# Ten more pairs of column tiles by seven products, half-set sums spread over two blocks and stored from ScalarE's queue, in a gated four-branch layer (one core, Trainium2)

## The chip, the cores and the metric

The kernel runs on one core of one Trainium2 chip. The metric is the device time of one execution in microseconds (us); lower is better. The kernel before takes 2374.32 us, median of three runs (2374.21 to 2376.05).

## The reference, cut to what matters

```python
h = rmsnorm(x, g_pre[l])
proj = h @ w_in[l]                      # 1024 -> 12 parts of 512, and 4 x 1024 gate logits
(a_u, a_v, a_z, b_a, b_b, b_z, c_x, c_z, d_b, d_c, d_x, d_z, gate_logits) = jnp.split(proj, SPLITS, axis=-1)
v_n = layernorm(a_v, ...);  out_a = gmlp_spatial(a_u, v_n, w_s[l], b_s[l]) * silu(a_z)
out_b = silu(layernorm(causal_depthwise(b_a * sigmoid(b_b), conv_b_w[l]) + bias)) * silu(b_z)   # 31 taps
out_c = multiscale_pool(c_x) * silu(c_z)
out_d = d_b * causal_depthwise(d_c * d_x, conv_d_w[l]) * silu(d_z)                              # 3 taps
gates = sigmoid(gate_logits + b_gate[l])
merged = sum of gates[i] * (out_i @ w_branch[l, i]) over the four branches
y = merged @ w_out[l];  x = x + rmsnorm(y, g_post[l])
```

There is one layer, 2048 prompt tokens and 64 sample tokens, everything in float32. The tail of each state (conv, pool, short conv) and v_n of the sample are outputs too.

## The kernel before, in words

**Blocks and passes.** The 2048 tokens are worked in four blocks of 512; the last carries the 64 sample tokens as well, 576 columns. (The title of the change counts blocks from one: its blocks one and two are `j` = 0 and 1 here.) Every float32 operand is split into a high and a low part of type float32r, and each product takes three matmul passes: high by high, high by low, low by high.

**Units.** A block is 120 units in twelve sections (`SECTIONS`): B 8, V 4, C 8, M 8, G0 16, D 16, G1 16, G2 12, Z 4, G2b 4, G3 16, O 8. A full unit is one 128-column output tile of the input projection, 8 k tiles by 3 passes = 24 matmuls of 512 columns (48 of 288 in the last block). In a gated section (name with G) even units are gate logits, full; odd units are half units, 12 matmuls with a branch weight. `run_unit` (L1925) does a unit. Units alternate between the two PSUM halves `acc[:, 0]` and `acc[:, 1]`, and a unit waits until its half is emptied (`acc_free`): for gate units by ScalarE's sigmoid (L843), for half units by VectorE's merge (L1506).

**Weights.** In block 0 SyncE loads raw weights, ScalarE casts the high part (L776), GpSimd subtracts the low part (L643), and SyncE stores both in DRAM (`split_main`, `split_branch`). In later blocks SyncE loads the split weights into a ring of four (L502), each load issued when the unit four before it is done.

**Seven products.** In blocks 2 and 3 pairs of output tiles are worked as 2 by 2 block products in Strassen's manner (`seven_pairs`, `product`, L2146): 7 products of 12 matmuls with half the columns each, in place of two full units. `PAIRS` lists them: 25 per block, in G0 (the last three of four), D, G1, G2, Z, G3. The four partial sums of a pair are put together by VectorE (`pair_sums`, L1539 to L1554) in the tiles `zc`, beginning with a copy by ScalarE (`copy_p1`, L801). In D every odd pair stands in the `side` PSUM banks, the other pairs in `acc`. A product whose bank is used again waits for the sum that empties it: the sixth product of a pair waits for the first sum of the same pair.

They need sums on both sides. **Weight side, half sets:** each pair has two half sets, so 50. In block 1 SyncE loads a half set (L568), GpSimd makes four sums (L658 to L663; `s_half`), ScalarE casts the high part (`s_cast`, L787), GpSimd subtracts the low part (L666), and SyncE stores 1 MB in `s_parts` (L573). There are two output buffers, so the sums of a half set wait for the store of the one two before it, and three raw buffers. The tables `HALF_LOAD`, `HALF_CAST`, `HALF_STORE` and `HALF_POOL` say at which unit or pair of units each step stands in each engine's order. **Token side:** `t_sums` (L1406 to L1410) makes t1 to t4 from `h_hi` and `h_lo` by ten VectorE operations between the results of section M, ScalarE casts them (`t_cast`, L792), VectorE subtracts (`t_low`, L1418); the first pair waits for each.

**Order.** All orders are written out by hand. VectorE also works the 31 taps of the depthwise conv, one `conv_step` (L1197) of four operations (eight in the last block) at a time, put in wherever the code calls it. In block 0 SyncE, GpSimd and, in the gated sections, ScalarE run loops.

```python
HALF_LOAD = [h * 29 // 25 for h in range(NH)]
HALF_CAST = [max(0, 2 * s - 1) for s in HALF_LOAD]
HALF_STORE = [s + 2 for s in HALF_LOAD]
```

Of the kernel before, what the change touches and what calls it, by code (L numbers as in the profile page):

```python
# [19 lines left out]
P = 128  # L20
# [31 lines left out]
SEVEN = [("G0", 3), ("D", 8), ("G1", 4), ("G2", 4), ("Z", 2), ("G3", 4)]  # L52
PAIRS = [(n, q) for n, c in SEVEN for q in range(c)]
PAIR_TILE = [MAIN0["G2b"] if (n, q) == ("G2", 3) else MAIN0[n] + 2 * (q + (n == "G0")) for n, q in PAIRS]
# [5 lines left out]
SEVEN_AT = UNIT0["G0"] + 4  # L60
SEVEN_UNITS = UNIT0["O"] - SEVEN_AT
SEVEN_SIGS = 42
# [23 lines left out]


def half_unit(u):

    r = u % UPB  # L90
    return any(n[0] == "G" and UNIT0[n] <= r < UNIT0[n] + c and (r - UNIT0[n]) % 2 for n, c in SECTIONS)
# [40 lines left out]
def chunk_stream():  # L132
# [7 lines left out]
    for j in range(SEVEN0, NBLK):  # L140
        if j > SEVEN0:
            for name, count in SECTIONS:
                for r in range(4 if name == "G0" else count):
# [4 lines left out]
                if name == "G0":  # L148
                    break
        for p, (name, q) in enumerate(PAIRS):  # L150
# [4 lines left out]
            if name[0] == "G":  # L155
                srcs += [("branch", GATED[name][0] * KT + 2 * (q + (name == "G0")) + t, 0) for t in range(2)]
# [17 lines left out]
def build(nc, x_t, x_rows, w_main, w_half, w_branch, cols, rows, bs_rows, ws_t, mask_t, pool_w, ident_in,  # L174
# [82 lines left out]
    tmp = sb("tmp", [P, WMAX])  # L257
    diag_hi = sb("diag_hi", [P, BLK // P + 1, P], F32R)
# [5 lines left out]
    lnv_g_bc, lnv_b_bc = w_raw[0][:, 0:WB], w_raw[0][:, WB:2 * WB]  # L264
# [18 lines left out]
    for j in range(SEVEN0, NBLK):  # L283
        hw = (WMAX if j == NBLK - 1 else BLK) // 2
        part = CT * hw * 4
        if j == NBLK - 1:
            t_at = [raw_at, raw_at + part, xr_at, raw_at + 2 * part] + [xr_at + n * part for n in (1, 2, 3)] + [bs_at]
        else:
            t_at = [raw_at + n * part for n in range(4)] + [xr_at + n * part for n in (2, 3, 0, 1)]
# [197 lines left out]
    def _(sp):  # L487
        def raw_load(u, r, src, n):

            if not isinstance(u, int) or u >= RING:  # L490
                sp.wait_ge(w_lo_done, u - RING + 1)
            sp.dma_start(w_raw[r % RING][:, 0:n], src).then_inc(w_landed[r % RING], 16)

        def split_store(u, r, dst, n):

            sp.wait_ge(w_lo_done, u + 1)
            sp.dma_start(dst, f(w_pair[r % RING])[:, :, 0:n]).then_inc(split_stored[r % RING], 16)
# [18 lines left out]
        raw_load(0, 0, raw_rows(MAIN0["B"]), DM)  # L516
        load_x(sp, 0)

        for name, count in SECTIONS:
            u0 = UNIT0[name]  # L520
            prev = [n for n, _ in SECTIONS][max(0, [n for n, _ in SECTIONS].index(name) - 1)]

            def store_before(u, r, i):

                if i > 0 or not isinstance(i, int):
                    owner, m0 = name, i * 4 - 4
                elif name == "B":
# [24 lines left out]
            body(0)
            if name == "B":
# [1884 lines left out]
```

## Time and profile before

| what | value |
|---|---|
| median of the runs | 2374.32 us |
| the profiled execution: its own time | 2372.68 us |
| its span | 2370.9 us, 34948 instructions |
| PE (TensorE) busy | 2353.2 us, 99% |
| VectorE, GpSimd, ScalarE busy | 1563.9 (66%), 639.9 (27%), 442.7 us (19%) |
| PE in the chain that ended last | 92% |
| mean DRAM traffic | 290 GB/s |
| SyncE's DMA queue, ScalarE's DMA queue | 652.18 MB, 32.49 MB |

How to read it: PE is busy nearly all the time and its granted clock is full throughout, so the time is the sum of PE's instructions and of the few places where it stands still. Another engine matters only where it makes PE wait.

### The profile page before, as it was taken

Reading aid. Unit: us, or ns where it says so; the run is one execution under the profiler, and the core shown is the slowest. Engines: PE = TensorE matmul, PEld = TensorE weight load, DVE = VectorE, ACT = ScalarE, POOL = GpSimd, SP = SyncE. Lnnn points to the kernel's source line nnn. Section 1 sums busy time; section 2 is a strip of 40 time slices with the busy share of each in tenths; the row PEclk is TensorE's granted clock in tenths of the full one; section 3 lists DMA queues with packets and bytes.
Section 4 is the critical chain, followed back from the end, with each engine's and each line's share of the span. In section 5 each row is a group of like instructions: output and inputs, shape, how many; then the busy total and the mean of one; then the engine's idle time right before and its main releaser. Section 6 shows DMA issues by size and latency. Waiting matters only on the chain.

```text
span 2370.9 us, 34948 instructions
## 1 busy us (share of the span) xinstructions
PE 2353.2 (99%) x13240; PEld 2086.4 (88%) x13240; DVE 1563.9 (66%) x2349; ACT 442.7 (19%) x646; POOL 639.9 (27%) x423
## 2 busy tenths in 40 slices
PE   9999999999999999999999999999999999999998
PEld 7888888888888888788888899999899999999998
DVE  7886886854666578875276856776337786577643
ACT  5222222323112111121101100111110110010111
POOL 4534544455645646666200000000100000000000
PEclk9999999999999999999999999999999999999999
DMA  8877879788987988999764699999774458988884
GB/s 329 321 248 278 309 258 328 279 289 335 394 323 286 359 327 328 379 340 361 287 242 179 214 327 369 311 326 326 269 252 161 159 187 286 331 282 268 279 282 176
DMA packets 220673, 686.62 MB, mean 290 GB/s; under 512 B 18096, under 2 KB 19760, under 8 KB 186736
## 3 DMA queue, kind: packets, MB, share of 16 engines
q1 hardware_dynamic: 207920, 652.18, 76.9%
q10 hardware_dynamic: 12608, 32.49, 3.7%
q8 instruction: 93, 1.52, 0.2%
q14 instruction: 52, 0.43, 0.1%
HBM read 514.14 MB, written 170.46 MB: 289 GB/s over the span
## 4 chain that ended last, share of the span: by engine, by line
PE 92%; DVE 5%; DVEq 1%; DMA 1%; issue 1%; ACT 0%; POOL 0%; POOLq 0%; SPq 0%; ACTq 0%
PE acc L1925 50%; PE acc L2146 18%; PE side L2157 7%; PE side L2069 4%; PE side L2146 4%; PE acc L2306 3%; PE side L2306 3%; DMA w_pair<-split_main 1%; PE acc L2303 1%; PE side L2303 1%; PE side L2097 1%; PE side L2087 1%; DVE t_sum L1410 0%; PE acc L2336 0%; DVE cb L1197 0%
## 5 line engine op out<-in xcount | busy, mean ns | idle before, releaser
L1925 PE MATMUL acc<-h_hi,w_pair 128*128 128x512 f32 x2752 | 864.2, 390 | 3.5 <-DMA w_pair<-split_main 3.4
L1925 PEld LDWEIGHTS acc<-h_hi,w_pair 128*128 128x128 f32 x2752 | 516.7, 188 | 111.4 <-issue 3.8
L1925 PE MATMUL acc<-h_lo,w_pair 128*128 128x512 f32 x1376 | 535.3, 389 | 0.0
L1197 DVE SCALAR_TENSOR_TENSOR cb<-glu,col,cb 128x512 f32<-128x512 f32 x600 | 425.5, 775 | 18.5 <-issue 10.5
L643 POOL TENSOR_TENSOR w_pair<-w_raw,w_pair 128x1024 fp32r<-128x1024 f32 x118 | 268.4, 2286 | 272.6 <-ACT w_pair L776 257.5
L675 POOL TENSOR_TENSOR rstd<-msq,nhalf 128x5 f32<-128x5 f32 (+4 forms) x19 | 19.9, 1047 | 1125.5 <-DVE msq L1107 531.8
L1925 PEld LDWEIGHTS acc<-h_lo,w_pair 128*128 128x128 f32 x1376 | 258.4, 188 | 53.4
L2146 PE MATMUL acc<-t_hi,chunk 128*128 128x256 f32 (+1 forms) x1344 | 266.9, 287 | 1.3 <-DVE merged L1502 1.3
L2146 PEld LDWEIGHTS acc<-t_hi,chunk 128*128 128x128 f32 x1344 | 216.6, 189 | 1.9 <-DVE merged L1502 1.7
L2146 PE MATMUL acc<-h_hi,chunk 128*128 128x256 f32 (+1 forms) x1008 | 205.0, 289 | 2.4 <-issue 1.3
L2146 PE MATMUL acc<-t_lo,chunk 128*128 128x256 f32 (+1 forms) x672 | 193.1, 287 | 0.0
L1925 PE MATMUL acc<-out_hi,w_pair 128*128 128x512 f32 x528 | 173.6, 390 | 0.0
L2146 PEld LDWEIGHTS acc<-h_hi,chunk 128*128 128x128 f32 x1008 | 164.5, 190 | 4.0 <-DVE zc L1539 1.8
L666 POOL TENSOR_TENSOR s_out<-s_sum,s_out 128x1024 fp32r<-128x1024 f32 x50 | 122.5, 2449 | 150.9 <-ACT s_out L787 148.8
L2157 PE MATMUL side<-out_hi,chunk 128*128 128x288 f32 (+1 forms) x720 | 162.0, 327 | 0.0
L1925 PE MATMUL acc<-h_hi,chunk 128*128 128x288 f32 x832 | 146.9, 297 | 0.0
L2146 PE MATMUL acc<-h_lo,chunk 128*128 128x256 f32 (+1 forms) x504 | 145.3, 288 | 0.0
L776 ACT ACTIVATE w_pair<-w_raw 128x512 fp32r<-128x512 f32 (+1 forms) x117 | 109.8, 940 | 94.6 <-PE acc L1925 65.2
L2146 PEld LDWEIGHTS acc<-t_lo,chunk 128*128 128x128 f32 x672 | 126.9, 189 | 0.2
L2157 PEld LDWEIGHTS side<-out_hi,chunk 128*128 128x128 f32 x720 | 116.3, 188 | 8.9
L1925 PEld LDWEIGHTS acc<-h_hi,chunk 128*128 128x128 f32 x832 | 123.0, 189 | 0.5
L1925 PEld LDWEIGHTS acc<-out_hi,w_pair 128*128 128x128 f32 x528 | 99.1, 188 | 21.0 <-DVE tmp L1506 0.3
(327 smaller groups left out, 3409.2 us busy)
## 6 DMA issues: line engine op xcount, KB each, us to landing
w_pair<-split_main SPq DMA_DIRECT2D x118, 1024.0 KB, 6.3
chunk<-split_main SPq DMA_DIRECT2D x226, 512.0 KB, 5.6
chunk<-s_parts SPq DMA_DIRECT2D x200, 512.0 KB, 6.0
split_main<-w_pair SPq DMA_DIRECT2D x88, 1024.0 KB, 6.4
s_parts<-s_out SPq DMA_DIRECT2D x50, 1024.0 KB, 5.8
w_raw<-in_w_main SPq DMA_DIRECT2D x88, 512.0 KB, 4.6
chunk<-split_branch SPq DMA_DIRECT2D x62, 512.0 KB, 4.4
s_raw<-in_w_half SPq DMA_DIRECT2D x50, 512.0 KB, 6.6
```

What stands on the lines that cost most here:

```text
L643: pool.tensor_tensor(w_lo[s][:, 0:n], w_raw[s][:, 0:n], f(w_hi[s])[:, 0:n], ALU.subtract).then_inc(w_lo_done, 1)
L666: pool.tensor_tensor(s_out[h % 2][:, :, 1, :], s_sum[h % 2][:, :, 1, :], f(s_out[h % 2])[:, :, 0, :], ALU.subtract).then_inc(s_lo_done, 1)
L776: act.activation(w_hi[s][:, 0:n], w_raw[s][:, 0:n], ACT.Copy).then_inc(w_hi_done, 1)
L1197: dve.scalar_tensor_tensor(dst, src, c1("conv_w", c * CK + t), dst, ALU.mult, ALU.add)
L1925: ins = pe.matmul(acc[:, s, b, 0:m], w_k[:, wt, wk], mv_[:, k, t0:t0 + m], start=(k == 0 and n == 0), stop=(k == nk - 1 and n == 2))
L2069: ins = pe.matmul(v_tile(t), ht[:, k, t * P:(t + 1) * P], w_k[:, wt, :], start=(r == 0 and n == 0), stop=(r == 3 and n == 5))
L2087: ins = pe.matmul(side[:, k % 2, t0:t0 + m], wt[:, c, :], part[:, c, t0:t0 + m], start=(n == 0), stop=(n == 2))
L2097: ins = pe.matmul(side[:, k % 2, t * P:t * P + n], v_n[0:n, t, c * P:(c + 1) * P], ws[0:n, c, 0:n], start=True, stop=True)
L2146: ins = pe.matmul(bank, w_k, rhs[r_part][:, k, :], start=(k == 0 and c == 0), stop=(k == CT - 1 and c == 2))
L2157: ins = pe.matmul(side[:, m % 2, t * 512:t * 512 + m_], wt[:, w_part, k * P:(k + 1) * P], rhs[:, k, t0:t0 + m_], start=(k == 0 and c == 0) ...
L2303: ins = pe.matmul(bank[:, 0:N1], wt[:, part, n * P:(n + 1) * P], act_part[:, TOK * P:WMAX], start=(k == 0 and c == 0), stop=(k == KT - 1 a ...
L2306: ins = pe.matmul(bank, act_part[:, n // 2 * P:(n // 2 + 1) * P], wt[n % 2][:, part, :], start=(k == 0 and c == 0), stop=(k == KT - 1 and ...
```

## The change

1. `SEVEN` gains section M (4 pairs) and the first pair of G0: 30 pairs per block, ten more over blocks 2 and 3. The eight units of M and the first four of G0 are no longer run there. `seven_m` works M's results; the gMLP side products (`m_job`) move between the third and fourth product of M's pairs; the pool side products (`p_job`) move ahead, after units 2, 3, 6 and 7 of C.
2. There are 60 half sets. Sixteen (`HALF0`) are made in block 0, one buffer set, every 10.5 half units; the other 44 in block 1, on 50 of 54 slots of two units, with four slots from `X_ROWS_AT` (units 78 to 85, in G2) left free.
3. Their stores are issued by ScalarE: in `s_cast`, at the unit after the slot, behind the cast that stands at the same unit.
4. `t_sums` now makes t1 to t4 from `h_x` at the end of the block before, four operations, ahead of the casts, the low parts and GpSimd's `h_lo`, which overwrites `h_x` and so waits for them. The low parts follow before the statistics of `y_nat`.
5. Conv steps of blocks 2 and 3: 8 in B, 3 in C, 8 in G0, one in each of the first three D results (19 to 21), then as before. Block 0's loops on SyncE, GpSimd and ScalarE are written out. t4's high part lives in another place in the last block, with one copy of it by ScalarE.

```diff
-SEVEN = [("G0", 3), ("D", 8), ("G1", 4), ("G2", 4), ("Z", 2), ("G3", 4)]
+SEVEN = [("M", 4), ("G0", 4), ("D", 8), ("G1", 4), ("G2", 4), ("Z", 2), ("G3", 4)]
...
-HALF_LOAD = [h * 29 // 25 for h in range(NH)]
-HALF_CAST = [max(0, 2 * s - 1) for s in HALF_LOAD]
-HALF_STORE = [s + 2 for s in HALF_LOAD]
-HALF_POOL = [2 * s for s in HALF_LOAD]
+HALF0 = 16
+X_ROWS_AT = UNIT0["G2"] // 2 + 1
+SLOTS = [s for s in range(54) if not X_ROWS_AT <= s < X_ROWS_AT + 4]
+HALF_SLOT = [SLOTS[h * len(SLOTS) // (NH - HALF0)] for h in range(NH - HALF0)]
+SUM0 = [unit_at(26 + h * 21 // 2) for h in range(HALF0)]
+CAST0 = [unit_at(START[u] + 2) for u in SUM0]
+LOW0 = [u + 1 for u in CAST0]
+LOAD0 = [unit_at(START[u] - 8) + 7 for u in SUM0]
+HALF_LOAD = LOAD0 + [UPB + 2 * s for s in HALF_SLOT]
+HALF_STORE = [u + 1 for u in LOW0] + [UPB + 2 * s + 1 for s in HALF_SLOT]
+HALF_CAST = CAST0 + [UPB + max(0, 2 * s - 1) for s in HALF_SLOT]
+RAW_OF = [0 if h < HALF0 else (h - HALF0) % 3 for h in range(NH)]
+SUM_OF = [0 if h < HALF0 else (h - HALF0) % 2 for h in range(NH)]
...
+        def s_store(h):
+            act.wait_ge(s_lo_done, h + 1)
+            act.dma_start(s_parts[h // 2, h % 2, :, :, :, :], f(s_out[SUM_OF[h]])).then_inc(s_stored[SUM_OF[h]], 16)
         def s_cast(j, u):
+            for h in range(NH):
+                if HALF_CAST[h] == u:
+                    out, b = s_out[SUM_OF[h]], SUM_OF[h]
+                    act.wait_ge(s_summed, h + 1)
+                    act.activation(out[:, :, 0, :], s_sum[b][:, :, 1, :], ACT.Copy).then_inc(s_hi_done, 1)
+            for h in range(NH):
+                if HALF_STORE[h] == u:
+                    s_store(h)
...
+        def t_sums(j):
+            if j == SEVEN0:
+                for b in range(2):
+                    dve.wait_ge(s_stored[b], 16 * SUM_OF.count(b))
+            dve.drain()
+            dve.tensor_tensor(t1, b12, b11, ALU.subtract).then_inc(t_summed, 1)
+            dve.tensor_tensor(t3, b12, b22, ALU.subtract).then_inc(t_summed, 1)
+            dve.drain()
+            dve.tensor_tensor(t2, b22, t1, ALU.subtract).then_inc(t_summed, 1)
+            dve.drain()
+            dve.tensor_tensor(t4, b21, t2, ALU.subtract).then_inc(t_summed, 1)
...
+            def seven_m(c):
+                p = PAIRS.index(("M", c))
+                pair_sums(p, lambda: m_side(c))
+                dve.tensor_tensor(tmp[:, 0:w], tmp[:, 0:w], zc[0][:, 0:w], ALU.mult)
+                dve.wait_ge(pair_sig, sigs_before(j, p) + 1)
+                dve.tensor_tensor(tmp[:, 0:w], tmp[:, 0:w], sig[0][:, 0:w], ALU.mult)
+                dve.tensor_tensor(tmp[:, 0:w], tmp[:, 0:w], zc[1][:, 0:w], ALU.mult)
+                dve.drain().then_inc(pair_used, 2)
+                result(j, 1, c)
...
+                if i < 3:
+                    conv_step(j, 19 + i)
                 pair_sums(p + 1)
```

**ScalarE, section G3 of block 1, before.** Each sigmoid empties a gate unit; between them stands the cast of a half set.

```order
L843 ACTIVATE sig_104<-acc,col 128x512 [waits sig_used,acc_done]
L787 ACTIVATE s_out_100<-s_sum_102 128x4x256 [waits s_summed]
L843 ACTIVATE sig_105<-acc,col 128x512 [waits sig_used,acc_done]
L787 ACTIVATE s_out_101<-s_sum_103 128x4x256 [waits s_summed]
L843 ACTIVATE sig_104<-acc,col 128x512 [waits sig_used,acc_done]
```

The same place in the changed kernel:

```order
L849 ACTIVATE sig_104<-acc,col 128x512 [waits sig_used,acc_done]
L786 ACTIVATE s_out_100<-s_sum_102 128x4x256 [waits s_summed]
L778 DMA s_parts<-s_out_101 128x2048 [waits s_lo_done]
L849 ACTIVATE sig_105<-acc,col 128x512 [waits sig_used,acc_done]
L786 ACTIVATE s_out_101<-s_sum_103 128x4x256 [waits s_summed]
L778 DMA s_parts<-s_out_100 128x2048 [waits s_lo_done]
```

The store of one half set now stands behind the cast of the next one.

**VectorE, last block, section D, between an even pair and the odd pair after it, in the changed kernel** (`ext`, `tmp`: the three taps; `cb`: the conv; `zc_110<-side,zc_111`: first sum of the odd pair). Before, the four `cb` rows shown (eight in all) were not there, and the first sum followed the copies.

```order
L1775 COPY halo_d<-ext_112 128x2
L1777 COPY smp_d<-ext_112 128x2
L1218 SCALAR_TENSOR_TENSOR cb<-glu,col,cb 128x512
L1218 SCALAR_TENSOR_TENSOR cb<-glu,col,cb 128x64
L1218 SCALAR_TENSOR_TENSOR cb<-glu,col,cb 128x512
L1218 SCALAR_TENSOR_TENSOR cb<-glu,col,cb 128x64
...
L1551 TENSOR_TENSOR zc_110<-side,zc_111 128x288 [waits chunk_done,p1_copied]
```

A conv step of eight operations has moved ahead of the odd pair's first sum.

**VectorE, end of block 1, in the changed kernel** (`h_x`: the scaled input of block 2; `y_nat`: this block's output, whose statistics came right after `h_x` before).

```order
L1142 SCALAR_TENSOR_TENSOR h_x<-h_x,col,h_row 128x512
L1176 TENSOR_TENSOR t_sum_1_148<-h_x 128x1024 [waits s_stored1,s_stored0]
L1177 TENSOR_TENSOR t_sum_3_154<-h_x 128x1024
L1179 TENSOR_TENSOR t_sum_2_151<-h_x,t_sum_1_148 128x1024
L1181 TENSOR_TENSOR t_sum_4_157<-h_x,t_sum_2_151 128x1024
L1164 TENSOR_TENSOR t_lo_3_153<-t_sum_3_154,t_hi_3_152 128x1024 [waits t_hi_done]
L1164 TENSOR_TENSOR t_lo_1_147<-t_sum_1_148,t_hi_1_146 128x1024 [waits t_hi_done]
```

The token sums have moved from section M of the block to the end of the block before it.

## Rows read from the trace of the kernel before

**Rows 1.** The page: each engine's busy time; engines of the chain.

```profile
PE 2353.2 (99%) x13240; PEld 2086.4 (88%) x13240; DVE 1563.9 (66%) x2349; ACT 442.7 (19%) x646; POOL 639.9 (27%) x423
...
PE 92%; DVE 5%; DVEq 1%; DMA 1%; issue 1%; ACT 0%; POOL 0%; POOLq 0%; SPq 0%; ACTq 0%
```

**Rows 2.** Stretches of time: A:B, us; busy of five engines; clock, DMA share, GB/s.

```profile
57.00:545.00 488.00, 487.62 (x2169) 403.89 (x2169) 358.55 (x399) 140.07 (x185) 237.31 (x109) 1.00 0.81 289
590.00:1125.00 535.00, 531.49 (x2362) 439.93 (x2361) 361.81 (x422) 102.89 (x135) 312.33 (x250) 1.00 0.91 344
1402.00:1481.00 79.00, 78.79 (x667) 78.58 (x666) 49.45 (x103) 5.62 (x12) 0.00 (x0) 1.00 1.02 368
```

**Rows 3.** The chain that ended last: start us, us, what.

```profile
1290.95 5.44 PE acc L1925 x24
...
1392.13 9.93 PE acc L2146 x84
...
1803.18 31.98 PE acc L1925 x240
...
1970.42 11.10 PE acc L2146 x84
```

**Rows 4.** Timeline of PE where it enters the pairs, blocks 2 and 3.

```profile
1344.90 0.35 PE L2146 MATMUL acc<-h_hi,chunk 128*128 128x256 f32 x1 [1.28 <-issue]
...
1348.58 0.38 PE L2146 MATMUL acc<-t_hi,chunk 128*128 128x256 f32 x1 [0.58 <-DVE merged L1502]
...
1938.35 0.40 PE L2146 MATMUL acc<-t_hi,chunk 128*128 128x288 f32 x1 [0.67 <-DVE merged L1502]
```

**Rows 5.** PE's timeline in block 1, where a split weight comes late.

```profile
985.58 0.47 PE L1925 MATMUL acc<-h_hi,w_pair 128*128 128x512 f32 x1 [3.37 <-DMA w_pair<-split_main]
```

**Rows 6.** Section D, timeline: PE enters an odd pair; VectorE at its first sum.

```profile
1421.74 0.28 PE L2146 MATMUL side<-h_hi,chunk 128*128 128x256 f32 x1
...
2021.09 0.29 PE L2146 MATMUL side<-h_hi,chunk 128*128 128x288 f32 x1
```

```profile
1425.59 0.42 DVE L1539 TENSOR_TENSOR zc<-side,zc 128x256 f32<-128x256 f32 x1
...
2025.70 0.45 DVE L1539 TENSOR_TENSOR zc<-side,zc 128x288 f32<-128x288 f32 x1
```

**Rows 7.** VectorE's timeline: a conv step in block 2 and in the last.

```profile
1304.43 2.74 DVE L1197 SCALAR_TENSOR_TENSOR cb<-glu,col,cb 128x512 f32<-128x512 f32 x4
...
1887.46 3.53 DVE L1197 SCALAR_TENSOR_TENSOR cb<-glu,col,cb 128x512 f32<-128x512 f32 x8
```

**Rows 8.** Timelines of GpSimd and ScalarE in G3 of block 1.

```profile
1099.31 2.39 POOL L666 TENSOR_TENSOR s_out<-s_sum,s_out 128x1024 fp32r<-128x1024 f32 x1 [2.19 <-DMA s_parts<-s_out]
1101.66 1.19 POOL L658 TENSOR_TENSOR s_sum<-s_raw 128x256 f32<-128x256 f32 x1
...
1105.02 0.74 POOL L663 TENSOR_TENSOR s_sum<-s_raw,s_sum 128x256 f32<-128x256 f32 x1
```

```profile
1105.76 0.69 ACT L843 ACTIVATE sig<-acc,col 128x512 f32<-128x512 f32 x1 [6.52 <-PE acc L1925]
1106.34 1.05 ACT L787 ACTIVATE s_out<-s_sum 128x1024 fp32r<-128x1024 f32 x1
```

**Rows 9.** Issue to landing: tile `s_out` from 1060 to 1125 us; DMAs issued 1196:1198.

```profile
DMA to landing us min/median/max: 5.0/6.2/8.7
```

```profile
w_pair<-split_main SPq DMA_DIRECT2D x1, 1024.0 KB, 6.0
out_y_rows<-x_half ACTq DMA_DIRECT2D x1, 1024.0 KB, 7.0
```

**Rows 10.** Start of block 2: the chain, and VectorE's timeline.

```profile
1168.53 43.54 PE acc L1925 x192
```

```profile
1146.99 2.45 DVE L1145 SCALAR_TENSOR_TENSOR h_x<-h_x,col,h_row 128x512 f32<-128x512 f32 x2 [1.39 <-DMA h_x<-in_x_t]
...
1307.25 1.23 DVE L1408 TENSOR_TENSOR t_sum<-h_hi 128x1024 f32<-128x1024 f32 x1
```

More of the change, by code:

```diff
@@ L142, in chunk_stream @@
             for name, count in SECTIONS:
-                for r in range(4 if name == "G0" else count):
+                if name == "M":
+                    break
+                for r in range(count):
                     u = j * UPB + UNIT0[name] + r
@@ L155, in chunk_stream @@
             if name[0] == "G":
-                srcs += [("branch", GATED[name][0] * KT + 2 * (q + (name == "G0")) + t, 0) for t in range(2)]
+                srcs += [("branch", GATED[name][0] * KT + 2 * q + t, 0) for t in range(2)]
             for src in srcs:
@@ L263, in build @@
     mean_wb = sb("mean_wb", [P, 2])
-    lnv_g_bc, lnv_b_bc = w_raw[0][:, 0:WB], w_raw[0][:, WB:2 * WB]
+    lnv_b_bc, lnv_g_bc = [zc[b][:, 0:WB] for b in range(2)]
     bs_at = at[0]
@@ new lines, in _ @@
+        units = [(name, r) for name, count in SECTIONS for r in range(count)]
+        for u, (name, r) in enumerate(units):
+            m = unit_pieces(name, r)[0][1]
+            if half_unit(u):
+                raw_load(u, raw_branch_rows(m), WB)
+            else:
+                raw_load(u, raw_rows(m), DM)
+            if u == 0:
+                load_x(sp, 0)
+            if u >= RING:
+                m = unit_pieces(*units[u - RING])[0][1]
+                if half_unit(u - RING):
+                    split_store(u - RING, split_branch_rows(m), WB)
+                else:
+                    split_store(u - RING, split_rows(m), DM)
+            sum_moves(u)
+            if u == RING - 1:
@@ L664, in s_half, with s_low, sum_steps @@
             pool.drain().then_inc(s_summed, 1)
+        def s_low(h):
+            out = s_out[SUM_OF[h]]
             pool.wait_ge(s_hi_done, h + 1)
-            pool.tensor_tensor(s_out[h % 2][:, :, 1, :], s_sum[h % 2][:, :, 1, :], f(s_out[h % 2])[:, :, 0, :],
+            pool.tensor_tensor(out[:, :, 1, :], s_sum[SUM_OF[h]][:, :, 1, :], f(out)[:, :, 0, :],
                                ALU.subtract).then_inc(s_lo_done, 1)
+        def sum_steps(step):
+            for h in range(NH):
+                if HALF_LOW[h] == step and h < HALF0:
+                    s_low(h)
+            for h in range(NH):
+                if HALF_SUM[h] == step:
+                    s_sums(h)
+                    if h >= HALF0:
+                        s_low(h)
         powers = [0]
@@ L734, in _ @@
             else:
-                for u in range(UNIT0["O"]):
+                for u in range(UPB):
                     if u == UNIT0["B"] + 1:
@@ L942, in _ @@
                 c = r // 4 * 2 + r % 2
+                if last and r == 2:
+                    act.wait_ge(vn_ready, j + 1)
+                    act.dma_start(v_s, lnv_g_bc[0:DEC, :]).then_inc(v_stored, 16)
+                if last and r == 3:
+                    act.wait_ge(v_stored, 16)
                 if r % 4 < 2:
@@ L955, in _ @@
             u0 = ub + UNIT0["M"]
-            for r in range(8):
+            for r in range(0 if is_seven(j) else 8):
                 u = u0 + r
@@ L1432, in _ @@
                 dve.drain().then_inc(side_free, 1)
+            for c in range(0 if is_seven(j) else CT):
+                u = ub + UNIT0["M"] + 2 * c
+                m_side(c)
                 ready_at(0, u // 2)
@@ L1442, in _ @@
                 result(j, 1, c)
[L1443 to L1449 removed]
+                if c % 2:
                     conv_step(j, 4 + c // 2)
@@ L1529, in merge @@
                 else:
-                    unrolled(dve, int(is_seven(j)), start, end, body)
+                    unrolled(dve, 0, start, end, body)
             def pair_sums(p, between=None):
```

389 lines of the change are left out of this document (162 added, 227 removed).

## The prediction

> **What bounds the kernel now.** I read the page first: PE is busy for 99% of the span and holds 92% of the chain; VectorE (66%), GpSimd (27%) and ScalarE (19%) are far from full [rows 1]. The granted clock is 1.00 in each stretch read [rows 2], so no change of clock enters the sum. Then the stretches of time: block 0's main part has 0.4 us without PE, block 1's has 3.5 us (535.00 less 531.49), section D of block 2 has 0.2 us [rows 2]. Then the chain, for what a unit and a pair cost PE: a full unit takes 5.44 us in block 2 and 31.98/5 = 6.40 us in the last block; a pair takes 9.93 and 11.10 us [rows 3]. The timelines give the stalls: 1.28 and 0.58 us where block 2 enters its first pair, 0.67 us in the last block [rows 4], and 3.37 us in block 1 where a split weight lands late [rows 5]. So the time is PE's instruction stream plus some 6 us of stalls. The change shortens the stream in blocks 2 and 3 and pays for it in block 1, in the chain that makes half sets.
>
> All sums start from the profiled execution's own time, 2372.68 us. The median of the runs is 1.64 us above it, and I add that at the end. 0.2% is 4.7 us, about what a measurement of this kernel can tell from no change.
>
> **Matmuls.** Four pairs of M and one of G0 replace ten full main tiles per block; branch matmuls (half as two products of the same columns) stay as they were. Block 2: 2 x 5.44 - 9.93 = 0.95 us a pair, five pairs, -4.8. Last block: 12.80 - 11.10 = 1.70, five pairs, -8.5 [rows 3]. Together **-13.2**.
>
> **Entry into the pairs.** Before, the first pair had to wait for token sums made in M and in the pair's own time: 1.28 + 0.58 us in block 2, 0.67 us in the last [rows 4], and small ones beside them of some 0.5 us in all (an estimate). Now the sums are made a block earlier. **-3.0**, at worst -1.0 if VectorE is what is late next.
>
> **Late weight in block 1.** Rows of x come in then beside half-set loads and stores, and PE stands 3.37 us [rows 5]. The four free slots take 6 MB out of just that stretch. **-3.5**, at worst 0.
>
> **Conv steps in D.** A step now stands ahead of an odd pair's first sum, and PE's sixth product waits for that sum. Last block: PE enters at 2021.09, so the sixth starts 5 x 11.10/7 = 7.93 us later, at 2029.0; the sum started at 2025.70 and takes 0.45 [rows 6]; behind a step of 3.53 us [rows 7] and some 0.15 us of gaps it ends at 2029.8. That is 0.8 us late, three times: 2.4. Block 2: needed at 1421.74 + 7.09 = 1428.8, done at 1425.59 + 2.74 + 0.42 + 0.15 = 1428.9 [rows 6, 7]: 0.1 x 3. **+2.7**; bounds 0 (VectorE reaches D earlier now that merges lie better) and 5.
>
> **Sixteen half sets in block 0.** Each is 4.10 us of sums (1101.66 to 1105.76) and 2.39 of low part on GpSimd and 1.05 on ScalarE [rows 8]. GpSimd: 237 + 16 x 6.5 = 341 of 488 us busy. DMA: 16 x 1.5 MB more, 289 + 52 = 341 GB/s, which is what block 1 carries now (344) with one stall [rows 2]. They have a single buffer and some 28 us each, so the store's time is hidden. What could show is a weight's low part waiting behind a sum: **+0.5**, bounds 0 and 5 (the bound by the 3.4 us stall of [rows 5]).
>
> **At no cost, and under what cover.** M's pairs take 9.93 us plus 0.89 of the side product; they read 7 x 0.5 MB in 10.8 us, 339 GB/s, under the 368 that D takes without stall [rows 2]; if that cover fails, 0.5 us a pair. VectorE drops ten sums per block (1.23 us and more each [rows 10]) for four, and loses conv steps in M to B and G0, where the gate units leave it room. At the block's end the sums follow the scaled input, which ends at 1149.4; four times 1.23 puts them at 1154.4, and GpSimd's low parts have until 1168.5, when PE begins the next block [rows 10]; if that is short, up to 5 us a block. Pool side products in C are ahead by one or two units, which their operands have as slack; 0 to 1 us.
>
> **The stores on ScalarE: the deciding term.** Follow one half set in block 1. ScalarE issues the store of half set h behind the cast of h+1. The sums of h+2 wait until that store has landed (two buffers), and the cast of h+2 waits for the sums. So one turn is cast, issue, landing L, 4.10 of sums, about 0.2 of signals: L + 4.3 us. Before, SyncE issued the store without waiting for any later cast, so this ring didn't exist; even so GpSimd once waited 2.19 us for a landing [rows 8]. Behind the cast on ScalarE stands the sigmoid that empties PE's half of PSUM. In gated sections a slot is 5.44 + 2.72 = 8.16 us of PE time [rows 3], so each slot puts the cast back by L + 4.3 - 8.16 = L - 3.86 us. In D and where full units stand a slot is 10.88 us and gives back 6.58 - L. A cast can be late by some 8.5 us before PE waits: it is due a slot ahead, 10.9 less the cast, the sigmoid and signals [rows 8]. In G3 seven slots stand on end; I take it 3.5 us late on entry and count five steps: 3.5 + 5(L - 3.86) - 8.5. In G1 and in G0 four steps: 4(L - 3.86) - 8.5 each.
>
> For L there are two rows near: the stores of this very stretch, issued by SyncE, took 5.0/6.2/8.7 us (least, median, most), and a 1 MB store on ScalarE's queue took 7.0 beside a 1 MB load of 6.0 [rows 9]. I take 6.3, nearest the median of the same stores. Then G3 gives 3.5 + 12.2 - 8.5 = 7.2, G1 1.3, and G0 about nothing, since a free slot lies nearer to it: **+8.5**. Bounds: L = 5.0 gives 1 (G3 alone, 0.7), L = 7.0 gives 22 (next part).
>
> A rule weighed against this: by the rows, SyncE's stores stand in the same queue as weight loads, and here the store may either pass them or share with them; 6.0 beside 7.0 is one case of sharing [rows 9]. The Trainium skill, page "DMA: Bandwidth & Descriptors", section "Issuing engines are not separate DMA queues", says that DMAs of any issuing engine run on the same 16 DMA engines and interleave, and that issuing from another one saves only issue time. By that rule the store gains nothing, and this case's pair of 6.0 and 7.0 us agrees.
>
> **Sum.** -13.2 - 3.0 - 3.5 + 2.7 + 0.5 + 8.5 = -8.0: 2364.7 on the profiled execution's base, **2366.3** on the median's.
>
> **Rivals.**
> - *A, short ring.* L is 5.4 or less since the store no longer stands behind queued weight loads. For: the least was 5.0 [rows 9]. Against: 344 to 368 GB/s of other traffic. Ring cost about 2: -14.5, **2360**. Chance 0.22.
> - *B, the forecast*, 2362 to 2370: 0.40.
> - *C, long ring, slower.* The store shares with a load in flight: 1 MB more at 344 GB/s is 3.0 us on top of 5.0, L up to 8.0. At L = 7.0 G3 gives 10.7, G1 and G0 4.1 each, and since 11.3 is above 10.88 the eight slots of D give nothing back and cost 0.4 each: 22, so **2380**. From L = 7.0 on it decides for slower than before by 0.2%. At L = 7.7 the same count gives 14.2 + 6.9 + 6.9 and 1.1 for each of eleven full slots: 40, **2398**. For: the 7.0 on that queue, the most of 8.7. Against: the median of 6.2. Chance 0.20. The rule of the page named above, read so that each store is slowed by the loads it now runs beside, is this case.
> - *D, traffic.* Ring short, but block 0 at 341 GB/s and M's pairs make PE wait for weights, 1 to 5 us more than I count, or the late weight of block 1 stays (+3.5) because the x rows alone cause it: **2370 to 2373**. Against: block 1 carried as much with one stall. Chance 0.13.
> - *E, matmul gain only.* Nothing waits anywhere: -19 and below, **2355**. Chance 0.05.
>
> **How the numbers follow.** The forecast is the likeliest case, B's middle. Faster by over 0.2% is below 2369.6: A, E, most of B: 0.60. Within: the top of B, D, the start of C: 0.18. Slower, over 2379.1: C from L = 7.0 on, and mishaps of VectorE at the new places: 0.22. The range goes from just under A's 2360 (2357) to C's beginning at L = 7.1 (2384), leaving out E and long rings, some 0.2.
>
> **What would show it.** Right: ScalarE waits for the sums (`s_sum`) in G0, G1 and G3 of block 1, GpSimd waits for `s_parts` before its sums, and PE waits for `sig` in G3 in steps of about 2.5 us; landing of `s_parts` near 6.3; pairs at 9.93 and 11.10 in M; stalls of 0.8 us before the sixth product of three odd pairs in the last block; no stall at 985 us and none at the first pair. Wrong: PE full in block 1's G3 (A or E), waits for `w_pair` or `chunk` (D), new idle time of PE in block 0 or at a block's start, none of which the sum has at more than 0.5 us.

## The result and the profile after

The changed kernel takes **2412.0 us** (median of four runs, 2409.4 to 2416.6) against 2374.3: the ratio is 1.0159, with an interval of 1.0146 to 1.0172. That is slower by 38 us where 8 us less was forecast, and outside the range (2357 to 2384). The profiled execution took 2416.6 us, its span is 2414.8.

The page of the kernel after, engines and chain, to be read beside [rows 1]:

```profile
PE 2362.4 (98%) x13360; PEld 2095.9 (87%) x13360; DVE 1602.1 (66%) x2407; ACT 447.1 (19%) x651; POOL 697.3 (29%) x473
...
PE 72%; DVE 9%; DMA 8%; POOLq 3%; issue 2%; POOL 2%; DVEq 2%; ACT 1%; ACTq 0%; SPq 0%
```

PE's busy time rose by 9.2 us where the shorter stream should have lowered it by 13.2. Its idle time rose from 17.7 (span less busy) to 52.4 us. DMA went from 1% to 8% of the chain, nearly all of it `s_parts<-s_out`, the landing of the half-set stores.

Where the time went, by the end of each block's output projection in PE's timeline (L2306 before, L2333 after):

| block | before, us | after, us | difference | predicted |
|---|---|---|---|---|
| 0 | 589.1 | 607.4 | +18.3 | +0.5 |
| 1 | 579.1 | 618.6 | +39.5 | +5.0 |
| 2 | 556.2 | 548.5 | -7.7 | -6.8 |
| last | 640.0 | 633.8 | -6.2 | -6.8 |

(Predicted: the terms put in their blocks. Block 1: -3.5 + 8.5. Block 2: -4.8, its entry -2.3, conv steps +0.3. Last block: -8.5, entry -0.7, conv steps +2.4.) Blocks 2 and 3 came as forecast. All of the error is in blocks 0 and 1, where the half sets are made.

What PE waited for in block 0 (first fence) and in block 1 (second): engine, line, releaser, us in total, times, longest.

```profile
PE acc L1949 <- DVE tmp L1518: 5.5, 2, 3.1
PE side L2111 <- DVE out_lo L1386: 3.9, 1, 3.9
```

```profile
PE acc L1949 <- ACT sig L849: 22.3, 7, 8.9
PE acc L1949 <- ACTq L942: 7.7, 2, 6.2
```

In block 1 PE stood 30.0 us, always for ScalarE; in block 0 it waited for VectorE. Counted back from the block's end by the time of a unit, the 30.0 us lie in five places: 7.7 at the results of V (L942), 5.0 in G0, 1.5 in G1, 8.9 in G2 and 6.9 in G3. Stretches of time (columns as in [rows 2]); the last two are the 14 us around and behind the end of the pause of 6.23 us in block 1:

```profile
57.00:545.00 488.00, 477.14 (x2087) 392.48 (x2088) 400.06 (x391) 147.81 (x192) 329.33 (x182) 0.99 0.87 325
...
590.00:1125.00 535.00, 511.15 (x2232) 420.47 (x2231) 316.61 (x403) 95.61 (x129) 256.79 (x215) 0.97 0.84 312
...
686.00:693.00 7.00, 6.04 (x14) 4.84 (x15) 2.67 (x4) 1.47 (x2) 5.77 (x6) 0.50 0.36 150
...
693.00:700.00 7.00, 7.00 (x32) 5.74 (x32) 6.30 (x10) 1.55 (x2) 3.09 (x2) 1.00 0.45 156
```

```profile
686.96 0.80 PE L1949 MATMUL acc<-h_hi,w_pair 128*128 128x512 f32 x1 [6.23 <-ACTq L942]
...
692.67 0.56 PE L1949 MATMUL acc<-h_lo,w_pair 128*128 128x512 f32 x1
...
693.52 0.40 PE L1949 MATMUL acc<-h_lo,w_pair 128*128 128x512 f32 x1
```

After the pause the granted clock is 0.50, the 1.2 GHz level, up to about 692.7 us, and back at 1.00, 2.4 GHz, behind it. A run of three 512-column matmuls takes 1.28 us at the low level (687.98 to 689.26) and 0.68 at the high one, so 5.7 us at the low level cost 2.7 us. The low stretches behind the eight pauses of 2.0 us or more last 3.3 to 5.9 us and so cost 1.6 to 2.8 us each, some 17 in all (an estimate from their lengths and the two rates). The mean clock is 0.97 over block 1 and 0.99 over block 0. Taken over the whole run PE's busy time is 2362.4 where 2353.2 - 13.2 = 2340.0 was due. Of these 22.4 us two or three are not the clock's: the same stream at full clock (the runs with ten and nine half sets in block 0 below) is busy for 2342.3 to 2343.5. **So 17 to 20 us went to the low clock behind the pauses**, beside 34.7 us of more idle time. That cost was in no term of the prediction.

Block 1's ring, in the timelines of GpSimd and ScalarE (ACTq is ScalarE's issuing) before the longest pause:

```profile
998.51 0.92 POOL L658 TENSOR_TENSOR s_sum<-s_raw 128x256 f32<-128x256 f32 x1 [4.58 <-DMA s_parts<-s_out]
...
1004.08 2.40 POOL L670 TENSOR_TENSOR s_out<-s_sum,s_out 128x1024 fp32r<-128x1024 f32 x1 [1.22 <-ACT s_out L786]
1012.00 0.75 POOL L658 TENSOR_TENSOR s_sum<-s_raw 128x256 f32<-128x256 f32 x1 [5.52 <-DMA s_parts<-s_out]
```

```profile
1002.94 1.06 ACT L786 ACTIVATE s_out<-s_sum 128x1024 fp32r<-128x1024 f32 x1 [7.77 <-POOLq L664]
1002.95 0.33 ACTq L778 DMA_DIRECT2D s_parts<-s_out  x1
...
1015.25 1.06 ACT L786 ACTIVATE s_out<-s_sum 128x1024 fp32r<-128x1024 f32 x1 [10.67 <-POOLq L664]
1015.26 0.33 ACTq L778 DMA_DIRECT2D s_parts<-s_out  x1
1015.63 1.46 ACTq L859 DMA_DIRECT2D x_half<-in_x_rows  x2
1017.12 4.39 ACTq L862 DMA_DIRECT2D x_dec<-in_x_rows  x4
1021.61 0.69 ACT L849 ACTIVATE sig<-acc,col 128x512 f32<-128x512 f32 x1 [5.30 <-issue]
```

```profile
1002.95 8.92 DMA s_parts<-s_out
```

```profile
1022.35 0.80 PE L1949 MATMUL acc<-h_hi,w_pair 128*128 128x512 f32 x1 [8.87 <-ACT sig L849]
```

The store is issued at 1002.95, behind the cast at 1002.94, and lands 8.92 us later; GpSimd waits 5.52 us for it, makes its sums, and only then the next cast can run at 1015.25. One turn is 12.31 us, the landing + 3.4, where PE's work for a slot is 8.16 (10.88 where full units stand, so even there nothing is given back). Behind that late cast ScalarE still has six issues of x rows (5.9 us), then the sigmoid at 1021.61 that lets PE go on. The rows of x that the free slots were to protect thus add to the lateness on ScalarE, where the prediction had looked at SyncE alone.

Landing of the stores, 610 to 1200 us:

```profile
DMA to landing us min/median/max: 3.9/8.3/11.5
```

Block 0, VectorE (first fence) and GpSimd beside it in the 10 us that end in PE's pause of 3.12 us:

```profile
339.83 8.07 DVE L1218 SCALAR_TENSOR_TENSOR cb<-glu,col,cb 128x512 f32<-128x512 f32 x4
348.25 0.69 DVE L1518 TENSOR_TENSOR tmp<-acc,sig 128x512 f32<-128x512 f32 x1 [0.34 <-issue]
```

```profile
340.49 2.39 POOL L643 TENSOR_TENSOR w_pair<-w_raw,w_pair 128x1024 fp32r<-128x1024 f32 x1 [3.50 <-ACT w_pair L770]
342.84 2.84 POOL L670 TENSOR_TENSOR s_out<-s_sum,s_out 128x1024 fp32r<-128x1024 f32 x1
345.64 1.71 POOL L643 TENSOR_TENSOR w_pair<-w_raw,w_pair 128x512 fp32r<-128x512 f32 x1
```

Four conv operations that take 2.74 us where GpSimd rests [rows 7] took 8.07 here: GpSimd's `s_out` operation of the half set stands between two of its own for the weights. The four took 0.75, 2.93, 2.88 and 1.75 us, and each of the last three ended 0.55 us behind the end of a GpSimd operation. In the same section of the kernel before such a step took 3.4:

```profile
336.51 3.42 DVE L1197 SCALAR_TENSOR_TENSOR cb<-glu,col,cb 128x512 f32<-128x512 f32 x4 [0.26 <-issue]
```

In section D of the last block, PE at the sixth product of odd pairs:

```profile
2048.72 0.40 PE L2174 MATMUL side<-h_hi,chunk 128*128 128x288 f32 x1 [0.63 <-DVE zc L1551]
...
2072.23 0.41 PE L2174 MATMUL side<-h_hi,chunk 128*128 128x288 f32 x1 [0.97 <-DVE zc L1551]
...
2095.40 0.40 PE L2174 MATMUL side<-h_hi,chunk 128*128 128x288 f32 x1 [0.62 <-DVE zc L1551]
```

The pauses at the entry of the pairs [rows 4] and the late weight [rows 5] are gone.

### The profile page after: what moved, and what is told of

It is laid out like the page before. It is cut to its first block, busy times and chain, and to the rows that moved or that the text cites. A ratio compares the mean times of both kernels' runs of the same rounds, so it can differ in the third digit from the quotient of the medians.

```text
span 2414.8 us, 34960 instructions
## 1 busy us (share of the span) xinstructions
PE 2362.4 (98%) x13360; PEld 2095.9 (87%) x13360; DVE 1602.1 (66%) x2407; ACT 447.1 (19%) x651; POOL 697.3 (29%) x473
## 4 chain that ended last, share of the span: by engine, by line
PE 72%; DVE 9%; DMA 8%; POOLq 3%; issue 2%; POOL 2%; DVEq 2%; ACT 1%; ACTq 0%; SPq 0%
PE acc L1949 28%; PE acc L2174 22%; PE side L2185 8%; DMA s_parts<-s_out 8%; PE side L2174 3%; PE side L2093 3%; PE acc L2333 2%; PE side L2333 2%; DVE cb L1218 2%; POOLq L659 1%; POOLq L664 1%; POOLq L662 1%; POOL s_sum L660 1%; PE side L2121 1%; PE acc L2330 1%
## 5 line engine op out<-in xcount | busy, mean ns | idle before, releaser
L1949 PE MATMUL acc<-h_hi,w_pair 128*128 128x512 f32 x2592 | 824.6, 394 | 30.9 <-ACT sig L849 22.5
L2174 PE MATMUL acc<-t_hi,chunk 128*128 128x256 f32 (+1 forms) x1520 | 300.6, 287 | 0.0
L2174 PE MATMUL acc<-h_hi,chunk 128*128 128x256 f32 (+1 forms) x1248 | 253.1, 289 | 0.4 <-DVE zc L1551 0.4
L2174 PE MATMUL acc<-t_lo,chunk 128*128 128x256 f32 (+1 forms) x832 | 239.3, 288 | 0.0
L2174 PEld LDWEIGHTS acc<-h_hi,chunk 128*128 128x128 f32 x1248 | 203.5, 190 | 1.2 <-DVE zc L1551 0.6
L670 POOL TENSOR_TENSOR s_out<-s_sum,s_out 128x1024 fp32r<-128x1024 f32 x60 | 152.7, 2545 | 94.7 <-ACT s_out L786 94.7
L2174 PE MATMUL acc<-h_lo,chunk 128*128 128x256 f32 (+1 forms) x624 | 179.9, 288 | 0.0
L2174 PEld LDWEIGHTS acc<-t_lo,chunk 128*128 128x128 f32 x832 | 157.1, 189 | 0.2
L2174 PEld LDWEIGHTS acc<-h_lo,chunk 128*128 128x128 f32 x624 | 118.2, 189 | 0.6
L1518 DVE TENSOR_TENSOR tmp<-acc,sig 128x512 f32<-128x512 f32 x48 | 33.2, 691 | 127.2 <-PE acc L1949 81.8
```

Of the source, the lines that this page charges most:

```text
L670: pool.tensor_tensor(out[:, :, 1, :], s_sum[SUM_OF[h]][:, :, 1, :], f(out)[:, :, 0, :], ALU.subtract).then_inc(s_lo_done, 1)
L1518: dve.tensor_tensor(tv(tmp, j), accv(1, j), tv(sig[r], j), ALU.mult).then_inc(acc_free[1], 1)
L1949: ins = pe.matmul(acc[:, s, b, 0:m], w_k[:, wt, wk], mv_[:, k, t0:t0 + m], start=(k == 0 and n == 0), stop=(k == nk - 1 and n == 2))
L2174: ins = pe.matmul(bank, w_k, rhs[r_part][:, k, :], start=(k == 0 and c == 0), stop=(k == CT - 1 and c == 2))
```

## The experiments

Each was timed in three rounds or more beside the kernel before (2374.3 to 2375.4 us). Block times come from PE's timeline as above.

### The store ahead of the next cast

```diff
-HALF_STORE = [u + 1 for u in LOW0] + [UPB + 2 * s + 1 for s in HALF_SLOT]
+HALF_STORE = [u + 1 for u in LOW0] + [UPB + 2 * s for s in HALF_SLOT]
```

> The changed kernel took 18.3 us more than before in block 0 (607.4 against 589.1), 39.5 more in block 1 (618.6 against 579.0), 7.7 less in block 2 and 6.2 less in block 3. Here the stores of block 1 stay on ScalarE's queue, but stand one unit earlier: at the unit of the slot itself, ahead of the next half set's cast instead of behind it. Block 0 is untouched. Ring theory (the store behind the next cast makes one half set wait for the landing of the last): the ring is cut, so PE's waits for sig (22.5 us) and the clock falls behind them go, block 1 takes 579 to 584 us, the kernel 2374 to 2380. Queue theory (the stores take 8.1 us on ScalarE's queue and the sums wait for the landing in any case): landing stays 8 us and block 1 stays over 605 us, the kernel over 2398.

Measured: 2372.95 us, ratio 0.9992 (0.9982 to 1.0001). Block 1 takes 577.1 us, block 0 still 607.6. Its store landing, 600 to 1200 us, and its stretch of block 1:

```profile
DMA to landing us min/median/max: 5.1/8.0/17.8
```

```profile
625.00:1170.00 545.00, 543.59 (x2414) 449.61 (x2414) 363.05 (x429) 98.26 (x132) 271.06 (x221) 1.00 0.87 327
```

One unit's shift of one instruction gives back 39 us. The landing is about as long as in the changed kernel (8.0 against 8.3 us at the median), and GpSimd still waits for it 19 times, but PE loses 1.4 us in the whole stretch. Queue theory falls: the length of the landing does nothing unless the ring makes it count.

### The stores back on SyncE

```diff
+            for h in range(HALF0, NH):
+                if HALF_STORE[h] == step:
+                    sp.wait_ge(s_lo_done, h + 1)
+                    sp.dma_start(s_parts[h // 2, h % 2, :, :, :, :], f(s_out[SUM_OF[h]])).then_inc(s_stored[SUM_OF[h]], 16)
```

(with `HALF_STORE` at 2 * (s + 2), in `sum_moves` of SyncE, and without them in `s_cast`)

> The changed kernel, but block 1's stores are issued by SyncE again, two slots behind as in the kernel before; block 0's stay on ScalarE. Ring theory: block 1 takes 579 to 584 us, as in the run with the store ahead of the cast, kernel 2374 to 2380, whatever the landing time is. Queue theory: landing falls from 8.1 to about 6 us here and here alone, and only this run loses the 39 us, the other keeps them. If both theories are wrong and 44 half sets beside other traffic are the cause, block 1 stays over 605 us in both.

Measured: 2373.87 us, ratio 0.9995 (0.9986 to 1.0005); block 1 takes 577.2 us. Landing:

```profile
DMA to landing us min/median/max: 4.1/5.6/12.7
```

Both halves of the theory hold, each by itself: the queue sets the landing (5.6 against 8.0 us), the order sets whether it costs. A pause of 1.16 us for a weight stands at 1002.6 us, with the four slots free.

### The ring, but on SyncE's queue

```diff
+                    if h + 1 < NH and HALF_CAST[h + 1] == HALF_CAST[h] + 2:
+                        sp.wait_ge(s_hi_done, h + 2)
```

(ahead of the wait for `s_lo_done` of the last experiment, `HALF_STORE` at 2 * s + 5)

> The changed kernel, with block 1's stores issued by SyncE but still held back until the next half set's cast is done (where the next slot follows at once): the ring of the change, on the other queue. Measured so far: landing in block 1 is 8.0 us on ScalarE's queue and 5.6 on SyncE's; cutting the ring takes 39 us out of block 1 on either queue. Ring with its length (one turn is landing + 4.3 us against 8.16 of PE's time a slot): at L = 5.6 three stretches are late by 4 or 5 slots of 1.7, at most 8.7 of the 8.5 that are free plus 3.5 in G3, so block 1 takes 579 to 588 us, kernel 2374 to 2384. Order-alone theory (a store behind the next cast costs what it cost, on whatever queue): block 1 stays over 605, kernel over 2398. SyncE held at the wait can also delay weights, which would show as PE waiting for w_pair.

Measured: 2383.14 us, ratio 1.0038 (1.0025 to 1.0050). Block 1 takes 585.7 us, 8.6 more than with the ring cut. Landing and PE's pauses in block 1:

```profile
DMA to landing us min/median/max: 4.7/4.9/15.4
```

```profile
951.86 0.50 PE L1955 MATMUL acc<-h_hi,w_pair 128*128 128x512 f32 x1 [1.34 <-DMA w_pair<-split_main]
...
996.26 0.50 PE L1955 MATMUL acc<-h_hi,w_pair 128*128 128x512 f32 x1 [3.27 <-ACT sig L855]
...
1005.15 0.47 PE L1955 MATMUL acc<-out_hi,w_pair 128*128 128x512 f32 x1 [1.55 <-DMA w_pair<-split_branch]
```

Against the block with the ring cut (577.1) the ring costs 9 us at a landing of 4.9 and 41 at 8.3 (618.6), and part of the 9 is SyncE, held at the new wait, bringing weights late (1.34 and 1.55 us). The turn behind the longest pause, from cast to cast on ScalarE:

```profile
981.32 1.06 ACT L792 ACTIVATE s_out<-s_sum 128x1024 fp32r<-128x1024 f32 x1 [6.62 <-POOLq L670]
...
991.67 1.06 ACT L792 ACTIVATE s_out<-s_sum 128x1024 fp32r<-128x1024 f32 x1 [8.71 <-POOLq L670]
```

That is 10.35 us, still over the 8.16 of a slot at a landing of 4.9, because SyncE's store waits for the end of the cast (issued at 982.41) where ScalarE's was issued at its start. So the ring is there on either queue, and costs by how far a turn, landing and the rest together, goes beyond a slot.

### Small sums in block 0

```diff
-            a11, a12, a21, a22 = (s_raw[RAW_OF[h]][:, c, :] for c in range(4))
-            s1, s2, s3, s4 = (s_sum[SUM_OF[h]][:, c, 1, :] for c in range(4))
+            n = 8 if 0 < h < HALF0 else HW
+            a11, a12, a21, a22 = (s_raw[RAW_OF[h]][:, c, 0:n] for c in range(4))
+            s1, s2, s3, s4 = (s_sum[SUM_OF[h]][:, c, 1, 0:n] for c in range(4))
```

(and the same width in the cast and in the low part; the rest of each of these half sets is left out)

> The changed kernel, but in block 0 the half sets after the first are summed, cast and lowered over 8 columns instead of 256 (the output is left incomplete there); all their DMAs, waits and places stay, block 1 is untouched. Contention theory (GpSimd's extra 100 us in block 0 slow VectorE's operations, several of 0.7 us took 2.2 to 4.5 there, and PE then waits for VectorE): block 0 takes 589 to 592 us, the kernel 2394 to 2398, VectorE's busy time falls by 15 us or more. Traffic theory (24 MB more of DMA in block 0 delay weights): block 0 stays at 605 to 608, the kernel at 2409 to 2413.

Measured: 2394.69 us, ratio 1.0086 (1.0066 to 1.0107). Block 0 takes 589.5 us, as in the kernel before, and its stretch reads:

```profile
57.00:545.00 488.00, 487.30 (x2168) 403.42 (x2167) 356.42 (x400) 143.02 (x201) 274.57 (x188) 1.00 0.91 339
```

VectorE's busy time there is 356.4 us where the changed kernel has 400.1, for the same work, and PE is back at 487.3 at full clock. The traffic is higher than in any other block 0 (339 GB/s, since the block is shorter) and costs nothing, so the traffic rival is out. The half sets' work stretches VectorE by 44 us, and 17.9 us of that reach PE (607.4 less 589.5), pauses and low clock together. ScalarE's casts are cut with GpSimd's operations, so the run alone does not tell these two apart; the timelines above, where VectorE's operations end with GpSimd's, do.

### Early store, ten half sets in gated sections

```diff
-HALF0 = 16
+HALF0 = 10
-SUM0 = [unit_at(26 + h * 21 // 2) for h in range(HALF0)]
+SUM0 = [unit_at(26 + h * 21 // 2) for h in (3, 4, 5, 9, 10, 11, 12, 13, 14, 15)]
```

> The changed kernel with the store ahead of the next cast, and with ten half sets in block 0 instead of sixteen: the ones in C, M and D (units 13, 18, 24, 49, 54, 59) are gone, those at units in gated sections stay; block 1 has 50 half sets in 50 slots. Ring and contention theories together: block 0 loses the waits for VectorE in C and D and takes 590 to 596 us, block 1 579 to 586, the kernel 2362 to 2374, below before. If block 1's ring is still there at full density, it shows as waits for sig and the kernel stays over 2380.

Measured: **2362.42 us**, ratio 0.9949 (0.9933 to 0.9966). Block 0 takes 593.2 us, block 1 577.4 with 50 half sets in 50 slots. One pause of the kind is left in block 0, 2.51 us at 424 us. The run has both fewer half sets in block 0 and only places in gated sections, so it does not show what either does alone. VectorE beside it:

```profile
410.05 0.69 DVE L1518 TENSOR_TENSOR tmp<-acc,sig 128x512 f32<-128x512 f32 x1 [0.16 <-issue]
410.89 2.70 DVE L1521 TENSOR_TENSOR merged<-merged,tmp 128x512 f32<-128x512 f32 x1
```

The multiply at L1518 reads PSUM and one tile and keeps its 0.69 us, in each of its 48 executions; the addition at L1521 reads two tiles in SBUF and took 2.70.

### Nine half sets, conv steps between the sums

```diff
-                if i < 3:
-                    conv_step(j, 19 + i)
-                pair_sums(p)
+                pair_sums(p, (lambda: conv_step(j, 19 + i)) if i < 3 else None)
```

(and `HALF0` 9 without the half set at unit 79, three free slots)

> The kernel with the early store and ten half sets in block 0 (2362.4), with the one at unit 79 moved to block 1 (nine in block 0, 51 slots in block 1, three left free for the rows of x) and the conv steps of D moved into the gap between the second and third sum of the even pair. Contention theory: the pause of 2.51 us at 424 us, where merge operations of 0.69 us took 2.7 beside GpSimd, goes with the low clock behind it: block 0 590 to 592 instead of 593.2. The three pauses of 0.62, 0.98 and 0.63 us in D of the last block go. Kernel 2356 to 2360. Rival: the conv step is then late for the third sum or the taps instead and the same 2 us show at another line, and three free slots bring the late weight back (+3): 2362 to 2365.

Measured: **2356.75 us**, ratio 0.9925 (0.9908 to 0.9942): it beats both kernels. Block 0 takes 591.2 us. The last block takes 630.8, 3.0 less than with the conv steps ahead of the odd pair's first sum (633.8), and no pause over 0.4 us is left in its D: before the third sum of the even pair, where the step now stands, VectorE had 2.65 us of idle time. Block 1 takes 578.8, 1.3 more, with a pause of 1.41 us for a sigmoid.

### The same ten, stores by SyncE

> The kernel with ten half sets in block 0, but block 1's stores issued by SyncE two slots behind, as before the change, instead of by ScalarE ahead of the next cast. If who issues the store is worth nothing by itself once the ring is cut: 2360 to 2365, as its twin (2362.4), with landing 5.6 instead of 8.7 us and no other effect. If the own queue takes load off SyncE's: this one is slower by 3 us or more, with PE waiting for w_pair in block 1.

(The edit is that of the stores back on SyncE, with ten half sets.) Measured: 2364.08 us (the median of five, one of which took 9941 us), ratio 0.9958 (0.9942 to 0.9973), landing 5.0 us at the median. Block 1 takes 579.2 us against 577.4, most of it one pause:

```profile
990.78 0.47 PE L1953 MATMUL acc<-h_hi,w_pair 128*128 128x512 f32 x1 [3.15 <-DMA w_pair<-split_main]
```

The medians are 1.7 us apart, less than the 3 of the rival, and the intervals of the two kernels overlap: that ScalarE's issuing is worth anything once the ring is cut is shown by this pause in the profiled executions, not by the times.

### No free slots

```diff
-SLOTS = [s for s in range(54) if not X_ROWS_AT <= s < X_ROWS_AT + 4]
+SLOTS = list(range(54))
```

> The kernel with the early store on ScalarE's queue and ten half sets in block 0 (2362.4), but without the four slots left free for the rows of x: the 50 half sets of block 1 are spread over all 54 slots. With the four slots free PE waited 0 us for a late weight here, but 3.15 us in the twin with the stores on SyncE's queue. Free-slot theory (the prediction's): the late weight comes back near 980 us, 2 to 4 us, kernel 2364 to 2367. Own-queue theory (what freed the weights is that the 1 MB stores no longer stand in SyncE's queue ahead of them): no pause over 1 us there, kernel 2361 to 2363, or below if the spread loosens the stores' landing.

Measured: 2366.23 us, ratio 0.9963 (0.9949 to 0.9977), 3.8 more than its twin by the medians, with intervals that overlap. The profiled execution has 2.5 us more in block 1, in small pauses for several releasers:

```profile
996.56 0.47 PE L1949 MATMUL acc<-h_hi,w_pair 128*128 128x512 f32 x1 [0.54 <-DMA w_pair<-split_main]
...
1002.97 0.50 PE L1949 MATMUL acc<-out_hi,w_pair 128*128 128x512 f32 x1 [0.69 <-DVE tmp L1518]
...
1052.01 0.50 PE L1949 MATMUL acc<-out_hi,w_pair 128*128 128x512 f32 x1 [0.73 <-ACT zc L1036]
```

Neither theory is met as written: the time lies in the range of the free-slot theory (2364 to 2367), but the late weight did not come back at its old size (0.54 us), so the own queue carries most of that. The free slots may be worth some 3 us in all, spread over small pauses.

## Why the prediction was wrong

- **Matmuls, -13.2: right.** The chain of the kernel after, in M of block 2 and D of the last block:

```profile
1343.06 9.94 PE acc L2174 x84
...
1353.89 9.94 PE acc L2174 x84
```

```profile
1976.43 11.12 PE acc L2174 x84
```

  From one pair of M to the next it is 10.83 us with the side product, as counted. Blocks 2 and 3 gained 13.9 us together; the terms make 13.5 (-13.2 - 3.0 + 2.7).
- **Entry, -3.0: right.** No pause is left there.
- **Conv steps in D, +2.7: right.** 0.63, 0.97 and 0.62 us are 2.2 in the last block (2.4 forecast), and nothing over 0.4 in D of block 2. Moved into a gap they cost nothing.
- **Late weight, -3.5: right in size, wrong in reason.** It went, but with SyncE's stores it stays at 1.16 and 3.15 us in spite of four free slots. Mostly the stores' leaving SyncE's queue took it away; the prediction gave all of it to the slots. That the number came out is luck.
- **Block 0, +0.5: the first step that failed**; it measured +18.3. The step said that what could show is a weight's low part behind a sum, and looked at GpSimd's and the DMA's load alone. The small-sums run shows what it was: VectorE's operations are stretched while GpSimd works. The trace of before held the sign, unread: in its block 0 a conv step beside GpSimd took 3.4 us, and 2.74 without, and from 57 to 545 us its 120 conv operations took 1086 ns each at the mean (1269 in the changed kernel). The Trainium skill, page "SBUF — State Buffer", section "Who interferes with whom", says that a VectorE instruction with two SBUF inputs contends with a GpSimd instruction that reads SBUF, and that one with at most one SBUF input, outside some modes, does not. With that the trace agrees: L1521, with two SBUF operands, took 2.70, and L1518, with one in PSUM, 0.69.
- **The ring, +8.5: the mechanism right, the size off, above all by its L.** The step took L = 6.3 as "nearest the median of the same stores"; those were stores on the other queue. On ScalarE's queue the median was 8.3. The row that had the right queue, 7.0 us [rows 9], was in hand, and was only one transfer. The trace of before had more of them, which the prediction did not read: six 1 MB stores on ScalarE's queue at a median of 8.4, beside the half-set stores on SyncE's at 5.8.

```profile
s_parts<-s_out SPq DMA_DIRECT2D x50, 1024.0 KB, 5.8
...
out_y_rows<-x_half ACTq DMA_DIRECT2D x6, 1024.0 KB, 8.4
```

  A turn was L + 3.4 where L + 4.3 was taken. The places were off too: in G3 and G1, where the count had 7.2 and 1.3 us, PE stood 6.9 and 1.5; the other 21.6 us came in G0 (5.0), at V (7.7), where full units were to give time back, and in G2 (8.9), behind the x rows, and for these three the sum had nothing. By the prediction's own count L = 8.4 gives 57 us, more than came, so its slack and steps are not shown to be right, and that G3 and G1 came out near is partly luck. The range was cut at L = 7.1 and rival C at 0.20; at L = 7.7 rival C gave 2398, which is 40 us for the ring where block 1 lost some 43 to it (39.5, and the 3.5 of the late weight that it gained). That nearness is luck as well: the 40 are pauses alone, and the 43 are 30.0 of pauses and 12.9 of slower matmuls.
- **"No change of clock enters the sum": the second step that failed.** It was read from a kernel in which PE hardly stood, and the change made it stand. In block 1 the pauses grew by 26.6 us (30.0 less 3.4) and the block by 39.5, so 12.9 are matmuls that ran slower: five times the clock fell, at 1.6 to 2.7 us each, which makes some 11 of them. In block 0 the pauses are 10.0 us and the block lost 18.3, with three falls.

Put together: 17.8 us in block 0 (18.3 less 0.5), 34.5 in block 1 (39.5 less 5.0) and -0.4 in the two others are the 51.9 by which the profiled execution's 2416.6 missed the 2364.7 forecast for it.

What stays open is why a 1 MB store takes 8 us on ScalarE's queue and 5 to 5.6 on SyncE's. The prediction's reading of its pair of 6.0 and 7.0 us, that the store gains or loses nothing by its queue, does not hold. Nor do the weight loads gain what the store loses: from 700 to 1150 us they took 7.3 us at the median with the stores on ScalarE's queue, and 7.4 and 6.5 in the two runs with sixteen half sets in block 0 and the others' stores on SyncE's. In block 1:

```profile
w_pair<-split_main SPq DMA_DIRECT2D x65, 1024.0 KB, 7.3
s_parts<-s_out ACTq DMA_DIRECT2D x36, 1024.0 KB, 7.9
```

```profile
w_pair<-split_main SPq DMA_DIRECT2D x63, 1024.0 KB, 7.4
s_parts<-s_out SPq DMA_DIRECT2D x36, 1024.0 KB, 4.9
```

(The first fence is the store ahead of the next cast, on ScalarE's queue, the second the ring on SyncE's: issues, KB each, median us to landing.)

## What to carry to other kernels

When an instruction is moved to another engine, write down what stands in front of it there, and follow the buffer that it frees back to the same engine: a store behind the next cast closed a ring of cast, store, landing and sums, and one unit's shift (a `+ 1` less in one table) opened it again for 39 us. Price a landing on the queue that will carry it, from all transfers of that queue in the trace, and price a wait of a full PE together with the slower clock that can follow it, here 1.6 to 2.8 us behind each of eight pauses. Work put on an idle GpSimd is not free for a busy VectorE: give it less, and place it where VectorE has room, as the ten half sets in gated sections, which gave back 14 of block 0's 18 us.

## What the runs showed of the hardware beyond what was expected

- The same 1 MB store from SBUF: 8.0 us to landing on ScalarE's queue and 5.6 (4.9 and 5.0 in two other runs) on SyncE's, at the same traffic of 327 and 328 GB/s from 625 to 1170 us.
- In the changed kernel each of the eight pauses of PE of 2.0 us or more was followed by some microseconds at 1.2 GHz (0.50 granted from 686 to 693 us behind 6.23 us). The pause of 3.37 us before [rows 5] was not, nor were those of 2.51 and 3.15 us in the two kernels with ten half sets in block 0: the granted clock of the 15 us behind each is 1.00. And with ten half sets and SyncE's stores a pause of 1.23 us, at 431 us, was followed by a granted clock of 0.72 over 431.12 to 435.00. So the length of a pause alone does not tell.
- VectorE's operations with two SBUF operands, 0.69 us, took up to 2.8 beside GpSimd. From 57 to 545 us of block 0 the changed kernel has 92 us more of GpSimd's busy time than the kernel before (329.3 against 237.3) and 41.5 us more of VectorE's (400.1 against 358.6).
